# Order of the gated branch products, and place of the last head's transposes, in a two-block model kernel

## What is computed

```python
# first block
branch = jnp.einsum('bsnc,ncd->bsnd', ys, w_branch[l])        # 4 branches, 256 -> 1024
gates = jax.nn.sigmoid(gate_logit.reshape(bsz, seq, N_BRANCH, D_MODEL))
x = x + jnp.sum(gates * branch, axis=2) @ w_out[l]
...
# retention mixer, second block; o is (B, S, 4 heads, 512)
o = o * lax.rsqrt(jnp.mean(o * o, axis=-1, keepdims=True) + RMS_EPS)
o = (o.reshape(B, S, h * dv) * jax.nn.silu(g.astype(jnp.float32))).astype(x.dtype)
return o @ w_out
```

## Time and profile before

| what | value |
|---|---|
| median of 3 runs | 1317.81 us (1317.24 to 1327.22) |
| the profiled execution | 1317.81 us |
| its span in the profile | 1315.7 us |
| TensorE busy in the span | 1228.0 us, 93% |
| branch stage, first matmul to first out product | 281.27 to 304.37 us |
| first retention-output product | from 680.28 us |

### The profile page before, as it was taken

One profiled execution on the slowest core, in us unless ns is written; L12 is line 12 of the kernel. 1 busy time (PEld: TensorE's weight loads), 2 busy tenths in 40 slices (PEclk: granted clock), 3 DMA queues, 4 the chain that ended last, 5 costly groups with the idle time before them and its releaser, 6 DMA issues.

```text
span 1315.7 us, 19049 instructions
## 1 busy us (share of the span) xinstructions
PE 1228.0 (93%) x7404; PEld 1084.9 (82%) x7404; DVE 778.9 (59%) x965; ACT 596.6 (45%) x827; POOL 175.6 (13%) x174
## 2 busy tenths in 40 slices
PE   6999999998899997999999799999798877999997
PEld 6899999997788886888888688887797756888875
DVE  5744754466788444545545677744875665777642
ACT  6635654343444333443444444433556644544431
POOL 1000000023232101211100222210101001222200
PEclk9989989999899998999999899999899888999999
DMA  9343334445355555345436355554343304455530
GB/s 351 117 154 129 137 136 153 171 156 192 128 192 189 210 191 199 132 157 181 171 128 224 140 187 186 186 201 171 136 161 129 128 1 159 160 189 178 185 118 32
DMA packets 32002, 212.00 MB, mean 161 GB/s; under 512 B 4197, under 2 KB 4861, under 8 KB 7624
## 3 DMA queue, kind: packets, MB, share of 16 engines
q1 hardware_dynamic: 28936, 201.68, 43.1%
q0 software_dynamic: 2720, 9.26, 2.0%
q10 hardware_dynamic: 288, 0.23, 0.1%
HBM read 210.08 MB, written 1.07 MB: 160 GB/s over the span
## 4 chain that ended last, share of the span: by engine, by line
PE 78%; issue 6%; DVE 6%; ACT 6%; POOL 2%; DMA 1%; SPq 0%; DVEq 0%; POOLq 0%; ACTq 0%
PE acc L370 41%; PE acc L449 17%; PE acc L451 9%; PE aux L370 5%; ACT ns L994 2%; ACT wh L343 1%; POOL gate L605 1%; PE acc L406 1%; PE acc L410 1%; PE acc L408 1%; DVE ns L1527 1%; DVE wl L351 1%; PE aux L503 1%; DMA raw<-in_stream 1%; PE aux L1929 1%
## 5 line engine op out<-in xcount | busy, mean ns | idle before, releaser
L343 ACT ACTIVATE wh<-raw 128x2048 fp32r<-128x2048 f32 x190 | 363.8, 1917 | 311.5 <-PE acc L370 186.4
L351 DVE TENSOR_TENSOR wl<-raw,wh 128x2048 fp32r<-128x2048 f32 x126 | 288.7, 2294 | 272.2 <-ACT wh L343 272.1
L449 PE MATMUL acc<-hx,wh 128*128 128x512 f32 x960 | 337.6, 398 | 0.8 <-DVE hx L1328 0.8
L451 PE MATMUL acc<-hx,wl 128*128 128x256 f32 x960 | 268.0, 279 | 0.0
L370 PE MATMUL acc<-hx,wh 128*128 128x256 f32 x1280 | 242.6, 292 | 4.9 <-DVE hx L518 2.4
L449 PEld LDWEIGHTS acc<-hx,wh 128*128 128x128 f32 x960 | 181.2, 189 | 45.2 <-issue 1.9
L370 PEld LDWEIGHTS acc<-hx,wh 128*128 128x128 f32 x1280 | 208.0, 200 | 8.8 <-issue 5.4
L358 DVE TENSOR_TENSOR wl<-raw,wh 128x1024 fp32r<-128x1024 f32 x128 | 164.4, 1285 | 37.1 <-ACT wh L343 36.9
L370 PE MATMUL acc<-hx,wl 128*128 128x256 f32 x640 | 185.3, 290 | 0.0
L451 PEld LDWEIGHTS acc<-hx,wl 128*128 128x128 f32 x960 | 181.7, 189 | 0.0
L370 PEld LDWEIGHTS acc<-hx,wl 128*128 128x128 f32 x640 | 127.4, 199 | 0.0
(11 more groups left out here) (303 smaller groups left out, 1811.6 us busy)
## 6 DMA issues: line engine op xcount, KB each, us to landing
raw<-in_stream SPq DMA_DIRECT2D x190, 1024.0 KB, 4.8
bias_b<-in_bias POOLq DMA_DIRECT2D x7, 512.0 KB, 3.8
grow<-in_grows POOLq DMA_DIRECT2D x4, 512.0 KB, 4.6
nbias<-strip POOLq DMA_DIRECT2D x4, 512.0 KB, 4.1
x<-in_x SPq DMA_DIRECT2D x2, 512.0 KB, 4.2
y<-x SPq DMA_DIRECT2D x1, 1024.0 KB, 4.0
decay<-in_decay POOLq DMA_DIRECT2D x1, 512.0 KB, 3.9
growb<-in_grows POOLq DMA_DIRECT2D x1, 512.0 KB, 3.6
```

Source lines behind the costliest of these rows:

```text
L343: nc.scalar.activation(wh[:, s, :], raw[:, s, :], ACT.Copy).then_inc(hi_ready, 1)
L351: nc.vector.tensor_tensor(wl[:, s, :], raw[:, s, :], wh[:, s, :].bitcast(F32), ALU.subtract).then_inc(lo_ready, 1)
L449: nc.tensor.matmul(out[:, :], wh[:, s, cols], hx[:, k].rearrange("p a n -> p (a n)"), start=(k == 0), stop=False, skip_group_check=True)
L451: last = nc.tensor.matmul(out[:, 0:SEQ], wl[:, s, cols], hh[:, k, :], start=False, stop=(k == KT - 1), skip_group_check=True)
```

## The change

Two edits, and no change in what is computed.

The first turns the branch stage round: the outer loop runs over branches `n`, the inner over column groups `j`, `m = 4n + j`. The chunks of the stream are cut to match (a chunk is one branch, all 1024 columns, two k tiles). The products use four banks in turn instead of eight, so product `m` waits for gating `m - 4`. The vector engine has one whole split per branch instead of two halves per column group. GpSimd adds branches 1 and 2 (eight additions), and the vector engine adds branch 3 (four additions) and hands the sum on. ScalarE makes its four weight splits before it rounds any of the sum. TensorE waits for all 16 gatings before the out stage instead of 12. The split of out chunk 2 is the last thing on the vector engine's list in the stage.

The second moves `turn_head` of head 3 from behind the first retention-output product to in front of it.

```diff
         def branch_bank(m):
 
-            return (aux[:, m % 8 - 4, :] if m % 8 >= 4 else
-                    (aux[:, 4, :], aux[:, 5, :], acc[0][:, :], acc[1][:, :])[m % 4])
+            return (aux[:, 4, :], aux[:, 5, :], acc[0][:, :], acc[1][:, :])[m % 4]
...
-            for j in range(4):
-                for n in range(1, 4 if j < 3 else 3):
-                    pool.wait_ge(branch_out, 4 * j + n + 1)
-                    if n > 1:
-                        pool.wait_ge(mix_sum, 2 * j + n - 1)
+            for n in range(1, 3):
+                for j in range(4):
+                    pool.wait_ge(branch_out, 4 * n + j + 1)
+                    if n == 2:
+                        pool.wait_ge(mix_sum, j + 1)
                     a, b = gate[:, 2 * j:2 * j + 2, :], gate[:, n * KT + 2 * j:n * KT + 2 * j + 2, :]
-                    g.tensor_tensor(a, a, b, ALU.add).then_inc(mix_sum if n < 3 else mix_ready, 1)
+                    g.tensor_tensor(a, a, b, ALU.add).then_inc(mix_sum, 1)
...
-            split_hi(act, START["branch"] + 3)
+            for i in range(4):
+                split_hi(act, START["branch"] + i + 3)
+
             for j in range(4):
-                if j < 3:
-                    split_hi(act, START["branch"] + j + 4)
                 act.wait_ge(mix_ready, j + 1)
                 a.activation(hh[:, 2 * j:2 * j + 2, :], gate[:, 2 * j:2 * j + 2, :], ACT.Copy).then_inc(norm_hi, 1)
...
-            for j in range(4):
-                for n in range(4):
-                    if n in (1, 3):
-                        split_lo_half(dve, START["branch"] + j + 3, n // 2)
-                    m = 4 * j + n
-                    if n < 3:
-                        dve.wait_ge(branch_done, 3 * j + n + 1)
+            for n in range(4):
+                for j in range(4):
+                    if j == 2 and n < 3:
+                        split_lo(dve, START["branch"] + n + 3)
+                    m = 4 * n + j
+                    if j < 3:
+                        dve.wait_ge(branch_done, 3 * n + j + 1)
                     else:
-                        dve.wait_ge(mm_done, START["branch"] + j + 1)
-                    if m == 0:
+                        dve.wait_ge(mm_done, START["branch"] + n + 1)
+                    if n == 0:
                         group_out(dve, GROUP["gates"] + 14)
                         group_out(dve, GROUP["gates"] + 15)
                     gg = gate[:, n * KT + 2 * j:n * KT + 2 * j + 2, :].rearrange("p k n -> p (k n)")
                     v.tensor_tensor(gg, gg, branch_bank(m), ALU.mult).then_inc(branch_out, 1)
-                    if n == 1 and j:
-                        mix_lo(j - 1)
-            dve.wait_ge(mix_sum, 8)
-            dve.wait_ge(branch_out, 16)
-            v.tensor_tensor(gate[:, 6:8, :], gate[:, 6:8, :], gate[:, 3 * KT + 6:3 * KT + 8, :], ALU.add).then_inc(mix_ready, 1)
+                    if n == 3:
+                        dve.wait_ge(mix_sum, 4 + j + 1)
+                        dve.wait_ge(branch_out, m + 1)
+                        aa = gate[:, 2 * j:2 * j + 2, :]
+                        v.tensor_tensor(aa, aa, gate[:, n * KT + 2 * j:n * KT + 2 * j + 2, :], ALU.add).then_inc(mix_ready, 1)
+                        if j:
+                            mix_lo(j - 1)
             mix_lo(3)
+            split_lo(dve, START["branch"] + 6)
...
-            for j in range(4):
-                c = At(START["branch"] + j)
+            for n in range(4):
+                c = At(START["branch"] + n)
                 take(pe, c)
                 s = c.mod(SLOTS)
-                for n in range(4):
-                    m = 4 * j + n
-                    wait(pe, branch_out, m - 7)
+                for j in range(4):
+                    m = 4 * n + j
+                    wait(pe, branch_out, m - 3)
...
-                            if j == 0 and sub == 0:
+                            if sub == 0:
                                 pe.wait_ge(ys_lo, 2 * n + k + 1)
-                            w = slice((2 * n + k) * CW + sub * P, (2 * n + k) * CW + (sub + 1) * P)
+                            w = slice(k * D + (2 * j + sub) * P, k * D + (2 * j + sub + 1) * P)
...
-                    last.then_inc(branch_done if n < 3 else mm_done, 1)
-            pe.wait_ge(branch_out, 12)
+                    last.then_inc(branch_done if j < 3 else mm_done, 1)
+            pe.wait_ge(branch_out, 16)
...
+            turn_head(RET_HEADS - 1)
             for cg in range(2):
                 for i in range(4):
                     product_w(pe, START["ret_out"] + 4 * cg + i, GROUP["ret_out"] + 2 * cg, yth, ytl, WKT * i, WKT, 2 * KT,
                               None if cg else lambda k: (yt_lo, k + 1))
-                    if (cg, i) == (0, 0):
-                        turn_head(RET_HEADS - 1)
...
-    ch += [np.concatenate([k_tiles(a["w_branch"][0, n], CW * j, 0, 2)[:, 0:2 * CW] for n in range(4)], axis=1) for j in range(4)]
+    ch += [k_tiles(a["w_branch"][0, n], 0, 0, 2, D) for n in range(4)]
```

## The result

The changed kernel takes 1328.47 us in the median of 20 runs (1321.35 to 1337.47), against 1319.14 us for the kernel before, also over 20 runs (1314.97 to 1327.22). The ratio is 1.0064, 95% interval 1.0046 to 1.0083: slower by 8.4 us, 6.1 to 10.9, of 1319. The ratio is the one on record for the comparison; the two medians alone are 9.3 us apart. The forecast was slower by 6.0 us.

What follows compares the result with a forecast made beforehand. TensorE, busy 93% of the span, was taken to bound the kernel. Retention gap 4.75, its slow clock 2.0 and first edit -0.8 made +6.0 us: 1317.8 + 6.0 = 1323.8 us, range 1318 to 1329.

Steps and rivals of the forecast that it cites:

- Second edit, the gap: Before the last head's transposes: TensorE idles 4.6 us until ry is ready, costing +4.75 us.
- Second edit, the clock: Behind the gap before the transposes: slow clock costs 2.0 us, range 0 to 3.6.
- First edit, no gaps among the branch products: Branch products on TensorE: four banks suffice, no wait between the 16 products, 0 us.
- First edit, the gap at the end: Before the out products: TensorE idles 3.6 us, from 304.5 to 308.1, until gating 15 is done.
- The bound with no collision: End of the branch stage: gating 15 done at 306.0 if GpSimd's additions do not get in the way.
- GpSimd additions still near 2.2 us: Branch stage: sign that the forecast is right, GpSimd's additions still taking near 2.2 us each.
- First edit, the second half: Out products' second half: starts at 320.2 instead of 319.12, without a gap, and ends at 331.1 instead of 331.9.
- First edit, the clock: Out products behind the new 3.6 us gap: a slow stretch, partly inside the gap, costs 1.2 us.
- The sum: Whole kernel: 4.75 + 2.0 - 0.8 = +6.0 us; the -0.8 us is the branch and out stages' share.
- the first rival: Branch stage's end costs +1.8 us, retention gap 4.75 and its clock 3.6: +10.2 us, 1328.0 us; chance 0.18.
- The slow stretches fall well: Rival: branch stage gives -2.5 us, retention gap costs 4.75 and 0.5: +2.8 us, 1320.6 us; chance 0.17.

Runs made afterwards that it cites:

- filled run: Kernel before with the second edit and 20 unused matmuls ahead of the transposes: 1320.28 against 1319.36 us, ratio 1.0005; repeated, 1322.79 against 1318.21, ratio 1.0034.
- unfilled: Kernel before with the second edit only, no filler matmuls: 1327.58 against 1319.36 us, ratio 1.0070.
- first edit alone: Changed kernel with turn_head of head 3 back in its old place: 1319.72 against 1319.36 us for the kernel before, ratio 1.0006.
- run with the gap of 2.96 us: Kernel before with the second edit, and a vector-engine split moved behind the last head's two multiplications: 1322.94 against 1320.30 us, ratio 1.0008.

## Why the prediction was right, and where it was off

- *Second edit, the gap.* Predicted 4.6 us before the transposes and +4.75 us for the stage. Measured 4.57 us, and 4.8 us in the filled run. The transposes were released by ry as predicted. That ry keeps its own pace held, and ry's last wait was the vector engine's split, as the rows said.
- *Second edit, the clock.* Predicted 2.0 us, from slow stretches behind two gaps of other lengths. Measured 2.4 us, filled against unfilled. That a slow stretch came at all was in part luck: behind a gap of 2.96 us at the same place there was none.
- *First edit, no gaps among the branch products.* Right, with four banks.
- *First edit, the gap at the end.* Predicted 3.6 us from gating 15 at 26.8 us behind the first branch matmul. Measured 3.36 us, with gating 15 done at 26.6 us. The bound with no collision was 24.7 us; without GpSimd's additions it came at 305.77 - 280.80 = 25.0 us. The collisions with GpSimd came as predicted, but smaller: two additions of 0.80 and 1.00 us and the low part of 1.78 us, where each takes 0.69 alone, make 1.5 us and not 2.1. The vector engine's own work was 0.3 us longer than the bound has it, so two small errors cancel.
- *A sign that did not come.* "GpSimd additions still near 2.2 us": in the changed kernel none is. Four take 1.29 us, two 1.73 and 1.74, and two 3.29 and 3.34 us, each begun about 0.15 us behind the start of a whole split:

```profile
L604 POOL TENSOR_TENSOR gate<-gate x8: 1283/1512/3341, 292.3 to 305.7; 128x512 f32<-128x512 f32 x8
```

  The three numbers are the shortest, the median and the longest, in ns. The eight still ended 23.4 us behind the first branch matmul; the prediction's 305.3 is 24.0.
- *First edit, the second half.* That it would start without a gap was right: the vector engine's addition into x ends at 324.17, the second half starts at 324.52, and TensorE has no gap between 310.65 and the end of the stage.
- *First edit, the clock.* This term was mis-sized: "Part of it falls in the gap, so I take 1.2 us". In the changed kernel's trace TensorE ran at 0.50 from 310.65 to about 316.8, which is 3.1 us of loss; in the first edit alone it ran so from 305.24 to 308.1, 1.4 us. The sum of -0.8 us became +0.9 us in the one and -0.6 us in the other. The prediction also took the slow stretch of before for a fixed saving of 1.9 us; in three of six traces of that stage it was not there.
- *The sum.* 6.0 us predicted, 8.4 us measured, 8.1 us by the two stages of the profiled pair. The place of each gap and the sign of the whole held; the first edit's own sign is open (+0.8 us in the runs, -1.8 to +3.6). In the pair the missing 2.1 us are slow clock, 1.9 us in the first edit and 0.4 in the second, less 0.2 us of gap. That this pair comes so near to the runs is luck: with before's stage at 49.0 us it would be 9.7 us. Over all runs, the 21 of the changed kernel and the 87 of before in the comparisons above, the changed kernel's mean clock is 0.9599, before's 0.9647; by 0.94 us for 0.001 that is 4.5 us of a difference in means of 9.1 us. In the pair 3.6 us more of slow clock stand in the two stages (2.4, and 3.1 against 1.9). The rest was not traced to a place.
- *The rivals.* The measured 8.4 us is nearer to the first rival's 10.2 than to the forecast's 6.0, so the forecast held by its range and not by its best value. That rival had the longer slow stretch in the branch stage right (1.9 us, measured 3.1 and 1.4) and the rest too dear: gating 15 at 28.6 us behind the first branch matmul (measured 26.6) and 3.6 us of slow clock behind the retention gap (measured 2.4). "The slow stretches fall well" is what the run with the gap of 2.96 us shows can happen.
- *What can be measured.* The prediction held that 0.5% could not be told from no change. With 20 runs of each the interval is 0.46% to 0.83%, clear of no change.

## What to carry to other kernels

When TensorE's wait for something is moved forward, read in the old trace when that input is ready: the new gap is that time less the time at which TensorE now gets there, and what stood between was its cover. A loop turned round can be free in itself and lose by what goes with it; here the new order with eight banks beat the kernel before by 4.1 us (1.1 to 7.3). Look at which weight split stands ahead of a hand-over to TensorE and is needed only later: moving one was worth 2.2 us of stage with the clock at full speed on both sides. Before a slow stretch is counted as a cost or a saving, look at the same stage in other traces.

## What the runs showed of the hardware

- Behind the same gap of 3.36 us, ended by the same instruction, TensorE's clock was 0.50 for 6.1 us after the restart in one kernel and for 2.8 us in another.
- In six traces of one unchanged stage with a gap of 1.88 to 1.92 us, a slow stretch came in three (0.50 from 320.7 to 324.0 in before's) and none in three; the stage took 50.6 or 49.0 us accordingly. Behind a gap of 2.96 us the clock stayed at 1.00, behind one of 1.76 us it fell. The length of a gap does not say what the clock costs; one profile is a sample of it.
- Time and mean granted clock go together, 0.94 us for 0.001, and single executions differ by more than the stages do: the filled kernel's two sets of 12 runs have medians of 1320.28 and 1322.79 us while the stage is 49 us in both traces. Comparing a stage between two rows decides what the medians of 12 runs don't.
- An addition of 512 columns on GpSimd took 1.29 us, and 2.20 us when a vector-engine split of 1.2 us had begun 0.16 us before it; moving that split away brought 1.29 us back. Begun about 0.15 us behind the start of a whole split it took 3.29 and 3.34 us. In the other direction a low part of 0.69 us took 1.78 us with a GpSimd addition of 1.73 us begun 0.51 us before it, and 0.69 us with GpSimd's additions left out. In both the extra time is in the duration of the operation that began later.
